# A gather of expert rows whose sequence runs on over the seams between token tiles

## What is computed

```
def one(args):
    hh, ee, gg = args
    a = jnp.einsum("tkd,td->tk", peer_down[ee], hh, preferred_element_type=jnp.float32)
    act = (gg * jax.nn.gelu(a)).astype(hh.dtype)
    return jnp.einsum("tk,tkd->td", act, peer_up[ee])
...
x = x + m_x[5] * _peer(h2, w_pq[l], peer_keys[l], peer_down[l], peer_up[l])
```

## Time and profile before

| | us |
|---|---|
| median of 3 runs | 4159.94 |
| lowest, highest | 4153.65, 4164.02 |
| the profiled execution | 4160.42 |
| its span in the trace | 4158.6 |

### The profile page before, as it was taken

One profiled execution on the slowest core, in us unless ns is written; L12 is line 12 of the kernel. 1 busy time (PEld: TensorE's weight loads), 2 busy tenths in 40 slices (PEclk: granted clock), 3 DMA queues, 4 the chain that ended last, 5 costly groups with the idle time before them and its releaser, 6 DMA issues.

```text
span 4158.6 us, 43344 instructions
## 1 busy us (share of the span) xinstructions
PE 3469.0 (83%) x14118; PEld 2193.7 (53%) x14118; DVE 2323.3 (56%) x4974; ACT 950.0 (23%) x1940; POOL 1509.0 (36%) x1757
## 2 busy tenths in 40 slices
PE   6999787888895887777688677767789979999999
PEld 2576443354462452333255522222259869798898
DVE  2313876444557776444423666666546676565564
ACT  1301111121111111221121111111123453334443
POOL 0000566555555666566600277667730000000000
PEclk8999899999997998898899899989999989999999
DMA  6575899989897999999922599989965414545444
GB/s 269 192 267 194 316 391 367 363 313 345 343 359 292 388 394 360 333 375 374 352 102 96 209 388 400 381 335 379 399 255 186 177 55 165 185 175 179 143 175 153
DMA packets 273452, 1156.77 MB, mean 278 GB/s; under 512 B 30849, under 2 KB 31617, under 8 KB 234370
## 3 DMA queue, kind: packets, MB, share of 16 engines
q0 software_dynamic: 221184, 805.40, 51.0%
q1 hardware_dynamic: 52098, 349.23, 22.8%
HBM read 1153.47 MB, written 1.05 MB: 278 GB/s over the span
## 4 chain that ended last, share of the span: by engine, by line
PE 50%; DMA 19%; issue 11%; DVE 11%; POOL 7%; ACT 2%; POOLq 0%; SPq 0%; DVEq 0%; ACTq 0%
DMA rows<-in_peer_up,iup 11%; PE ps L992 11%; DMA rows<-in_peer_down,idown 7%; PE ps L1045 7%; PE ps L1047 7%; PE ps L1046 7%; POOL rows L2504 4%; PE ps L711 3%; PE ps L879 3%; PE ps L922 3%; POOL rows L2439 3%; DVE rows L1984 2%; PE ps L899 2%; DVE rows L1933 1%; PE ps L951 1%
## 5 line engine op out<-in xcount | busy, mean ns | idle before, releaser
L992 PE MATMUL ps<-rows,diag 128*128 128x512 f32 x2048 | 968.0, 631 | 292.6 <-DMA rows<-in_peer_up,iup 287.9
L992 PEld LDWEIGHTS ps<-rows,diag 128*128 128x128 f32 x2048 | 405.9, 202 | 835.7 <-issue 593.0
L1984 DVE CUSTOM_DVE_ANT_0 rows<-rows,ps 128x1024 f32<-128x1024 f32 x512 | 615.0, 1220 | 413.7 <-DMA rows<-in_peer_down,idown 405.7
L951 PE MATMUL ps<-rows,diag 128*128 128x512 f32 x1024 | 511.7, 625 | 209.8 <-DMA rows<-in_peer_up,iup 159.5
L2504 POOL DMA_INDIRECT rows<-in_peer_down,idown x512 | 488.6, 954 | 400.4 <-PE ps L992 281.9
L2504 POOL DMA_INDIRECT rows<-in_peer_up,iup x512 | 483.3, 944 | 257.0 <-issue 110.6
L951 PEld LDWEIGHTS ps<-rows,diag 128*128 128x128 f32 x1024 | 176.6, 191 | 542.8 <-DMA rows<-in_peer_up,iup 365.8
L1045 PE MATMUL ps<-hT_hi,w_hi 128*128 128x256 f32 x1600 | 452.4, 283 | 8.9 <-DVE hT_lo L2095 8.9
L1047 PE MATMUL ps<-hT_lo,w_hi 128*128 128x256 f32 x1600 | 453.1, 283 | 0.0
L1046 PE MATMUL ps<-hT_hi,w_lo 128*128 128x256 f32 x1600 | 451.3, 282 | 0.0
L1933 DVE CUSTOM_DVE_ANT_0 rows<-rows,ps 128x1024 f32<-128x1024 f32 x256 | 309.2, 1220 | 210.7 <-DMA rows<-in_peer_down,idown 209.1
(11 more groups left out here) (315 smaller groups left out, 4298.2 us busy)
## 6 DMA issues: line engine op xcount, KB each, us to landing
wring<-in_wgu SPq DMA_DIRECT2D x66, 1024.0 KB, 4.7
wring<-in_wdn SPq DMA_DIRECT2D x33, 1024.0 KB, 4.8
wring<-in_wG SPq DMA_DIRECT2D x29, 1024.0 KB, 7.9
rows<-in_wmod SPq DMA_DIRECT2D x27, 1024.0 KB, 7.9
wring<-in_wpq SPq DMA_DIRECT2D x24, 1024.0 KB, 4.9
rows<-in_wgu SPq DMA_DIRECT2D x22, 1024.0 KB, 4.8
wring<-in_wmod SPq DMA_DIRECT2D x21, 1024.0 KB, 7.2
rows<-in_peer_down,idown POOLq DMA_INDIRECT x768, 6.4
```

The source lines that it names most:

```text
L951: ins = pe.matmul(ps[:, UPB + half, :], diag[:, j % DIAGS, :], rows[:, s, half * 512:(half + 1) * 512], start=(first and j == 0), stop=(la ...
L992: ins = pe.matmul(ps[:, UPB + half, :], diag[:, j % DIAGS, :], rows[:, j, half * 512:(half + 1) * 512], start=(first and j == 0), stop=(la ...
L1984: dve.tensor_tensor_reduce(out=rows[:, j, :], in0=rows[:, j, :], in1=h_ps, scale=1.0, scalar=0.0, op0=ALU.mult, op1=ALU.add, accum_out=a8[ ...
```

## The change

`JOINED = (1, 2, 3, 5)` names the tiles that join the one before. Into such a tile the sequence goes on: down 15, up 14, down 0 of the new tile, up 15 of the old one, down 1, up 0. What follows from it, engine by engine:
- GpSimd issues the old tile's up 15 as the partner of the new tile's group 0, with the old tile's indices.
- TensorE multiplies up 15 in the new tile's group 0. Ahead of up 0 of the new tile it waits for `sum_read` instead of "fin".
- ScalarE copies the new tile's tokens to `h_ps` (`tokens`) before the old tile's last diagonals.
- VectorE's `fin` is split into `sum_of` (the product, which signals `sum_read`) and `residual` (the addition). In tiles 1 to 3 the sum is read between the sixth and the seventh down row of group 1 (`SUM_AT = 6`), and the residual comes after the eighth. In tile 5 both come after the activation of group 0.
- In the slots beside c0 the norm of x1 and what follows it move two half-slots later (1 to 3), behind the residual that it reads.

```
+JOINED = (1, 2, 3, 5)
+SUM_AT = 6
...
-    place(1, k[0:4] + [("gpre", "x1", dp, j) for dp in range(3) for j in (1, 2)], 2)
+    place(3, k[0:4] + [("gpre", "x1", dp, j) for dp in range(3) for j in (1, 2)], 2)
...
-                def up(g, first=False, last=False):
-                    pos_ = 31 if last else 2 * g + 2
+                def up(g, first=False, last=False, G=G):
+                    pos_ = 31 if last and G + 1 not in JOINED else 2 * g + 2
+                    if first and G:
+                        pe.wait_ge(sum_read, G)
...
-                if n0 <= 1 < n1 and G:
-                    at_mark(pe, "fin", GATHERS[G - 1][0], GATHERS[G - 1][1] + 1)
-                groups(pe, n0, n1, lambda n: is_group(n, 0) or up(n - 1, first=is_group(n, 1)))
+                def group(n):
+                    if not is_group(n, 0):
+                        up(n - 1, first=is_group(n, 1))
+                    elif G in JOINED:
+                        up(GROUPS - 1, last=True, G=G - 1)
+
+                groups(pe, n0, n1, group)
                 run_stages(beside_b)
-                if n1 == GROUPS:
+                if n1 == GROUPS and G + 1 not in JOINED:
                     up(GROUPS - 1, last=True)
...
+                if n0 == 0 and G not in JOINED:
+                    tokens(G)
...
                 if n1 == GROUPS:
+                    if G + 1 in JOINED:
+                        tokens(G + 1)
                     diags(GROUPS - 1)
...
-                    if not first:
+                    if G or not first:
                         dve.wait_ge(diag_ready, 8 * g + P * G)
...
+                    if first and G in JOINED:
+                        sum_of(*GATHERS[G - 1])
+                        residual(*GATHERS[G - 1])
                     run_stages(stages_b)
...
                     for j in range(GROUP):
-                        dve.wait_ge(row_in[j], (16 * (32 * G + 1)) if first else 32 * g + 16 * (32 * G))
+                        if is_group(g, 1) and j == SUM_AT and G in JOINED:
+                            sum_of(*GATHERS[G - 1])
+                        dve.wait_ge(row_in[j], 16 if first and not G else 32 * g + 16 * (32 * G))
...
+                    if is_group(g, 1) and G in JOINED:
+                        residual(*GATHERS[G - 1])
...
+            def sum_of(run, t):
+
                 G = GATHER_NO[run, t]
                 for half in range(2):
                     at_evac(dve, ("bf", run, t, half))
                 dve.wait_ge(upp_done, P * (G + 1))
+                dve.tensor_tensor(mb[:, :], up_sum, mb[:, :], ALU.mult).then_inc(sum_read, 1)
+
+            def residual(run, t):
+                s = RUNS[run][0]
+                dve.wait_ge(sum_read, GATHER_NO[run, t] + 1)
+                dve.tensor_tensor(x[s][:, t, :], x[s][:, t, :], mb[:, :], ALU.add).then_inc(mark["fin"], 1)
+                at_mark(dve, "fin", run, t + 1)
...
                 offsets(idown[0], 0)
-                down(0, 0, 0, (idown[1], 1))
-                down(1, 1, 1, (iup[0], 0))
-                up(0, 0, ahead=(idown[0], 2))
+                if G in JOINED:
+                    down(0, 0, (iup[1], GROUPS - 1, idx[GATHERS[G - 1][1]]))
+                    up(GROUPS - 1, 1, ahead=(idown[1], 1), G=G - 1)
+                else:
+                    down(0, 0, (idown[1], 1))
+                down(1, 1, (iup[0], 0))
+                up(0, 0, ahead=(idown[0], 2))
...
-                up(m * 2, 0, ahead=(iup[1], GROUPS - 1))
-                up(GROUPS - 1, 1, True)
+                pair(GROUPS // 2 - 1, False)
+                if G + 1 not in JOINED:
+                    offsets(iup[1], GROUPS - 1)
+                    up(GROUPS - 1, 1, True)
```

More of the change, by code:

```diff
@@ L943, in by_turns, with up @@
                 G = GATHER_NO[run, t]
-                def up(g, js, first=False, last=False):
+                def up(g, js, first=False, last=False, G=G):
+                    if first and js[0] == 0 and G:
+                        pe.wait_ge(sum_read, G)
                     for j in js:
@@ L960, in group @@
                         up(n - 1, range(HALF, GROUP))
+                    elif G in JOINED:
+                        up(GROUPS - 1, range(HALF, GROUP), last=True, G=G - 1)
                     run_stages(stages_b)
@@ L1504, in gather @@
                         cols = slice(half * 512, (half + 1) * 512)
-                        act.activation(h_ps[:, cols], h[s][:, t, cols], ACT.Copy).then_inc(h_copied, 1)
+                        act.activation(h_ps[:, cols], h[RUNS[run][0]][:, t, cols], ACT.Copy).then_inc(h_copied, 1)
+                if n0 == 0 and G not in JOINED:
+                    tokens(G)
                 if beside_a or beside_b:
@@ L2023, in fin @@
                 dve.wait_ge(upp_done, P * (G + 1))
+                dve.tensor_tensor(mb[:, :], up_sum, mb[:, :], ALU.mult).then_inc(sum_read, 1)
[4 more added lines that the diff above has]
+                at_mark(dve, "fin", run, t + 1)
+            def fin(run, t):
+                s = RUNS[run][0]
+                G = GATHER_NO[run, t]
+                if G + 1 in JOINED:
+                    return
                 if run == "x1" and t == TT - 1:
+                    for half in range(2):
+                        at_evac(dve, ("bf", run, t, half))
+                    dve.wait_ge(upp_done, P * (G + 1))
                     for half in range(2):
@@ L2029, in fin @@
                 else:
-                    v(dve.tensor_tensor(mb[:, :], up_sum, mb[:, :], ALU.mult))
-                    dve.tensor_tensor(x[s][:, t, :], x[s][:, t, :], mb[:, :], ALU.add).then_inc(mark["fin"], 1)
+                    sum_of(run, t)
+                    residual(run, t)
                 at_mark(dve, "fin", run, t + 1)
@@ L2466, in by_turns @@
                 offsets(idown[0], 0)
-                if G == 4:
+                if G in JOINED:
+                    offsets(iup[1], GROUPS - 1, idx[GATHERS[G - 1][1]])
+                    group(0, 0)
+                else:
                     pool.wait_ge(upp_done, P * G)
-                pool.wait_ge(idx_copied, 2 * GROUPS * G + 1)
-                for j in range(GROUP):
-                    down(0, 0, j)
-                    if j == HALF:
-                        offsets(idown[1], 1)
-                        offsets(iup[0], 0)
+                    pool.wait_ge(idx_copied, 2 * GROUPS * G + 1)
+                    for j in range(GROUP):
+                        down(0, 0, j)
+                        if j == HALF:
+                            offsets(idown[1], 1)
+                            offsets(iup[0], 0)
                 group(1, 1)
@@ L2505, in fetch, with offsets, down @@
                                             in_offset=bass.IndirectOffsetOnAxis(ap=offs[:, j:j + 1], axis=0)).then_inc(row_in[j], 16)
-                def offsets(dst, g):
-                    src = idx[t][:, g * GROUP:(g + 1) * GROUP] if isinstance(g, int) else idx[t][:, bass.ds(g * GROUP, GROUP)]
+                def offsets(dst, g, of=idx[t]):
+                    src = of[:, g * GROUP:(g + 1) * GROUP] if isinstance(g, int) else of[:, bass.ds(g * GROUP, GROUP)]
                     pool.tensor_copy(dst[:, :], src).then_inc(idx_copied, 1)
-                def down(g, par, first=None, ahead=None):
+                def down(g, par, ahead=None):
                     for j in range(GROUP):
-                        if first == 0 and G:
-                            pool.wait_ge(upp_done, P * G - GROUP + j + 1)
-                        elif first == 1:
-                            pool.wait_ge(down_done, P * G + j + 1)
-                        elif first is None:
+                        if G == 0 and is_group(g, 1):
+                            pool.wait_ge(down_done, j + 1)
+                        elif G or not is_group(g, 0):
                             pool.wait_ge(upp_done, 8 * g + (P * G - 2 * GROUP + j + 1))
                         if j == 0:
-                            pool.wait_ge(idx_copied, 2 * g + (2 * GROUPS * G + (1 if first == 0 else 0)))
+                            pool.wait_ge(idx_copied, 2 * g + (2 * GROUPS * G + (1 if G == 0 and is_group(g, 0) else 0)))
                         fetch(A["peer_down"], idown[par], j)
@@ L2523, in down, with up @@
                             offsets(*ahead)
-                def up(g, par, last=False, ahead=None):
+                def up(g, par, last=False, ahead=None, G=G):
                     for j in range(GROUP):
```

35 lines of the change are left out of this document (18 added, 17 removed).

## The result

The changed kernel takes 4120.74 us (median of 4 runs, 4114.62 to 4121.74) against 4161.36 us of the kernel before (median of 4, one run more than in the table ahead, 4153.65 to 4164.02), a ratio of 0.9904 with a 95% interval of 0.989 to 0.9918. The profiled execution took 4121.74 us with a span of 4119.9 us; before it was 4160.42 us. So 38.7 us are gone between the two profiles, where 52.6 us were forecast.

A forecast was written before the change was run, and what follows sets the result against it. Row fetches bound quiet groups of tile 4, while each seam is held by waits of a different engine. The terms 7.5 + 18 + 11.4 + 15.7 = 52.6 us, off 4160, gave 4107 us; bounds 4090 to 4127, upper end 4133 with round trips.

The forecast's parts named there:

- The mechanism: At the four joined seams only waits go; every fetch, reduce, product and stage stays, in a new order.
- the signs: Expected evidence: seam stretches of 48 to 55 us (43 to 46 into tile 5), named idle gaps gone, quiet groups unchanged.
- Tile 1, 7.5 us: Seam into tile 1, set by TensorE: nearly both its gaps, 1.20 and 6.67 us, go; 7.5 us, bounds 5 and 14.5.
- Tile 2, 18 us: Seam into tile 2, set by VectorE, which also runs routing and the norm: 18 us gained, bounds 10 and 24.
- the hand-made order: Seam into tile 2, timed step by step: the eighth reduce after the norm ends at 1346, against 1363.47 before.
- Tile 3, 11.4 us: Seam into tile 3: TensorE's 10.30 us idle falls to 1 and up 0' shortens; 11.4 us, bounds 7 and 13.
- Tile 5, 15.7 us: Seam into tile 5, set by fetches: 18.7 us saved less 3 charged for the sum; 15.7 us, bounds 11 and 18.7.
- Residual against GpSimd's issue, 1.4 us inside the bounds: At four seams the residual pass slows a GpSimd fetch issue from 0.94 to 1.28 us, 1.4 us in all.
- The full queue: Rival: fetches never pause and seams cost no more than neighbouring groups; 70 us gained, about 4090 us; chance 12%.
- The round trip of 6.4 us: Rival: each seam pays one more fetch landing; 26 us of the gain go, 4133 us; chance 13%.
- The late h_ps: Rival: h_ps is ready only when TensorE finishes the old tile; time within 10 us of 4160; chance 5%.
- Starving weights: Rival: unpaused rows delay weight chunks at the seams, about 6.7 us each; sixteen give 4214 us; chance 3%.

The follow-up runs named there:

- Section 4: Changed kernel, but in tile 0's last group ScalarE copies the next tokens to h_ps ahead of its attention stage: 4115.12 us, ratio to the kernel before 0.9891.
- Section 2: Changed kernel, but TensorE makes the four broadcasts of tile 2's x1 norm ahead of up 0': 4108.24 us, ratio to the kernel before 0.9877.
- section 3: Changed kernel, but in tiles 1 to 3 four up 15 fetches alternate with the last four of down 0': 4118.86 us, ratio to the kernel before 0.9899.
- section 7: Changed kernel, but tile 5's routing stages leave group 0' free and begin in group 1': 4196.43 us on another chip, ratio to the kernel before 0.9896.
- section 5: Changed kernel, but in tiles 0 to 3 each up fetch stands between two down fetches, not in blocks: 4313.11 us, ratio to the kernel before 1.0369.
- section 8: Changed kernel with early norm broadcasts, early h_ps copy and fetches spread in tile 3's groups 10 to 15: 4174.89 us against 4238.8 before, ratio 0.9858.
- sections 6: Changed kernel, but up and down fetches alternate only in groups 10 to 15 of tile 3: 4182.28 us on another chip, ratio to the kernel before 0.9867.

## Why the prediction was right, and where it was not

*The mechanism.* The waits that were to go went at all four seams. VectorE's idle of 32 and 22 us ahead of the sum is gone, TensorE's gaps of 6.67 and 10.30 us are 2.20 and 1.99 us, the norm's group is the slowest of tile 2 (30.91 us), and quiet groups stay at 21.3 us in tile 4 and 24.4 against 24.0 in tile 3. TensorE does not wait for the sum ahead of up 0', and ScalarE's copy of h_ps holds VectorE at the first seam alone. One of the signs was put wrong: the stretch into tile 1 was to be 48 to 55 us and is 59.7, though the prediction's own 7.5 us off 67.8 would give 60.3. The forecast of 4107 was 13.7 us too low: 9.5 us are missing at the seams, 7.3 of them at tile 2, and the other 4.4 lie outside the seams.

*Tile 1, 7.5 us.* 6.9 measured. Section 4 confirms that TensorE bounds this seam: halving VectorE's idle time gives 2.9 us. The late copy of h_ps costs those 2.9 us; the forecast left some 0.4 us for it (7.87 less 7.5).

*Tile 2, 18 us.* 10.7 measured; this is the step that failed, in its size (the hand-made order itself gives 1363.47 - 1346 = 17.5 us). Counted from the first down fetch of 15, the hand-made order and the trace agree to the end of down 0' (46.0 forecast, 45.1 found). Then two terms of it were too small.

- "Up 15's last row is fetched after 1298.3, lands at 1304.8 and is multiplied by 1306.7" took up 15 as bound by its last row. It is bound by its first: GpSimd issues it behind the last fetch of down 0' (1281.83), it lands 6 us later (TensorE starts at 1287.98), and then TensorE needs 15.90 us for the eight rows, at a granted clock of 0.86 in the stretch. Up 15 ends 7.0 us later than forecast, and down 1', sum and residual some 5 us later.
- "The norm's broadcasts stand behind up 0' … which costs VectorE about 3 us": 6.85 us. Up 0' starts 6.9 us later than forecast and takes 15.77 us where I put 13.9, the price at the full clock. The rest of the norm is as forecast.

Section 2 removes the second and gets 6.0 us back, section 3 the first and gets 3.7 us; they overlap. With the broadcasts early the seam gives 16.7 us.

*Tile 3, 11.4 us.* 11.5 measured. The forecast 1 us of rest is 1.99 us, and up 0' is back at 13.97 us.

*Tile 5, 15.7 us.* 14.0 measured. The stretch is at 42.9 us, two groups of 21.4 us; the price of the sum in VectorE's row stands in the next group (24.8 against 20.2 us before), 4.6 us where I charged 3. VectorE there:

```profile
2683.82 1.23 DVE L2048 TENSOR_TENSOR mb<-ps,mb 128x1024 f32<-128x1024 f32 x1 [0.94 <-PE ps L955]
2685.08 1.23 DVE L2053 TENSOR_TENSOR x_in<-x_in,mb 128x1024 f32<-128x1024 f32 x1
2689.39 1.22 DVE L1950 CUSTOM_DVE_ANT_0 rows<-rows,ps 128x1024 f32<-128x1024 f32 x1
```

The wait for up 15 is the forecast 1 us, the two passes are 2.5 us, and the stage behind them takes 3.1 us, up to 2689.39; it was named but not charged. That it is the missing 1.6 us is not shown (section 7).

*Residual against GpSimd's issue, 1.4 us inside the bounds.* The residual of the seam into tile 3, and the fetch that GpSimd issues beside it:

```profile
1704.01 1.22 DVE L2053 TENSOR_TENSOR x_ctx<-x_ctx,mb 128x1024 f32<-128x1024 f32 x1
```

```profile
1704.10 1.94 POOL L2552 DMA_INDIRECT rows<-in_peer_up,iup  x1 [0.30 <-DVE a L2006]
```

The fetch begins 0.09 us behind the residual, takes 1.94 us instead of 0.94, and ends at 1706.04, 0.81 us behind the residual's end at 1705.23. The other three keep the same distance. Into tile 5 the residual is the second row of the fence above, ending at 2686.31, and the fetch

```profile
2685.51 1.61 POOL L2479 DMA_INDIRECT rows<-in_peer_up,iup  x1 [0.30 <-issue]
```

ends at 2687.12; into tile 1 a fetch of 1.04 us ends at 873.45, the residual at 872.64; and into tile 2 the residual runs from 1311.16 to 1312.38, with

```profile
1311.00 0.94 POOL L2552 DMA_INDIRECT rows<-in_peer_up,iup  x1 [0.30 <-issue]
1312.25 0.94 POOL L2552 DMA_INDIRECT rows<-in_peer_up,iup  x1 [0.30 <-issue]
```

where the first, begun ahead of the residual, takes its 0.94 us right through it, and the second begins 0.13 us before its end and loses nothing. So a fetch that begins within such a pass is held until the pass ends. The fetch of 1.28 us in the earlier trace rows is the same case, and the prediction paired it with the wrong pass: it began at 2660.22, ahead of the pass shown there (line 1909, at 2660.73), but within the one before it:

```profile
2659.47 1.23 DVE L1908 TENSOR_TENSOR shared<-shared,iota 128x1024 f32<-128x1024 f32 x1
```

It ends at 2661.50, 0.80 us behind that pass's end. The 14 traces of these kernels hold 398 fetches that begin 0.05 to 1.09 us into a pass of VectorE over two SBUF tiles of 128x1024, and every one ends 0.80 to 0.85 us behind the pass. The four residuals of the changed kernel cost 1.00 + 0.67 + 0.10 + 0 = 1.8 us, where I put 1.4. The Trainium skill ("SBUF — State Buffer", section "SBUF: two separate sides") has it that a VectorE pass with two SBUF inputs and a GpSimd operation that reads SBUF exclude each other, and that whichever starts first has the shared port for its whole instruction while the other blocks. The held fetches agree with it. The fetch of 1311.00 does not: it began first, and the residual beside it did not grow (1.22 us). What a fetch loses is set by where in the pass it begins.

*The rivals.* The full queue (all upper bounds, 70 us) is out: tiles 1 and 3 came near their central values. The round trip of 6.4 us, priced as a landing at each seam, is there in full at tile 2 alone, as the 7.15 us ahead of up 15. The late h_ps was real at the first seam (16.36 us of idle time on VectorE) and cheap (2.9 us), since another engine set the pace. Starving weights did not show: from tile 0 to tile 5 TensorE waits for weights once, for 6.6 us in the kernel before and 6.4 us in the changed one.

## What to carry to other kernels

An engine that fetches for two consumers takes its waits in order, so where its next fetch stands in the queue matters more than when the slot comes free; follow the first row of a block through it, not only the last. Work that stands behind a moved block on another engine (here the norm's broadcasts behind up 0') moves with it: look for the consumer that does not need that block and put it ahead. And a fine alternation of fetches that wins 3 us a group where the engines do only rows loses 3 us a group and more where they have stages, so make such a change by stretch and not by kernel.

## What the runs showed of the hardware

*The granted clock follows the order of fetches.* The same five groups of tile 3 have a granted clock of 0.83 in blocks and 0.98 spread (section 5): in blocks TensorE has a gap of 8.0 to 8.5 us ahead of every eight rows, and the clock changes within the group. From 1941 to 1949 us of the changed kernel's trace, a gap and the first 2.2 us of a block, it is 0.50 (1.2 GHz); from 1957 to 1965 us, the end of that block and the next gap, it is 1.00 (2.4 GHz). Spread, TensorE has a row every 2.6 us with gaps of 0.6 us, and four windows of 10 us from 2140 us on are all at 1.00. What the clock is worth here is an estimate: a block of eight up rows takes 15.9 us in these groups and 13.9 us at 2.4 GHz throughout, so at most 2 of the 3 us for a group. No run separates it from the order, and TensorE's busy time is no shorter when spread (80.63 against 80.58 us), since a row by itself takes 1.98 us; what shrank is its idle time.

*The transfers reach less on some chips.* The code of tile 4 is the same in all kernels here. Its thirteen quiet groups in the changed kernel take 276.88 us at 398 GB/s (section on the result). In the kernel of section 8, on one of the two other chips:

```profile
2350.28:2653.34 303.06, 212.34 (x421) 73.07 (x420) 182.15 (x428) 35.23 (x119) 201.64 (x235) 0.98 0.96 363
```

363 GB/s and 23.3 us for a group, with TensorE, VectorE and GpSimd as busy as ever; on the other one the same groups take 23.2 us each. On these chips the kernel before takes 1.9 and 1.8% longer (4239 and 4232 against 4159 us). Whether the chips themselves are slower or something beside this core used their memory, no run here shows. On such a chip an experiment whose gain ends at the transfers (sections 6 and 7) reads smaller. I had not expected it, and an absolute time of one chip can't be set beside that of another; a ratio can, if the bound is the same.
